# Two chained transformer blocks on one core: even start of the differential attention, earlier second scan, later last feed-forward product

## What is computed

```python
# first block, differential attention (8 heads, each with two score maps of width 64)
sc = jnp.einsum('bqhcd,bkhcd->bhcqk', qblk, k).astype(jnp.float32) * scale
p = jax.nn.softmax(sc, axis=-1)
w = (p[:, :, 0] - lambda_full * p[:, :, 1]).astype(v.dtype)
return jnp.einsum('bhqk,bkhe->bqhe', w, v)
# second block, one of its three branches (a gated linear scan, forward and backward)
q = jax.nn.silu(q_raw); f = lb + (1.0 - lb) * jax.nn.sigmoid(f_raw); k = (1.0 - lb) * jax.nn.sigmoid(-f_raw)
o_f = _hgrn2_scan(q, k[:, :, 0], v, log_f[:, :, 0])
o_b = _flip(_hgrn2_scan(_flip(q), _flip(k[:, :, 1]), _flip(v), _flip(log_f[:, :, 1])))
return _group_rmsnorm(o_f + o_b, norm_g, HG_H) * jax.nn.silu(g_out)
# second block, feed-forward
up = _dwconv(u @ w_up[l], ffn_conv_w[l], ffn_conv_b[l])
a_half, v_half = jnp.split(up, 2, axis=-1)
h = h + (jax.nn.silu(a_half) * v_half) @ w_down[l]
```

## Time and profile before

| | us |
|---|---|
| median of the 3 runs | 2515.18 (2513.99, 2515.18, 2522.87) |
| the profiled execution | 2519.92 |
| its span | 2518.1 |
| PE busy | 2456.8 (98%) |
| DVE, ACT, POOL busy | 1790.1 (71%), 1449.0 (58%), 258.8 (10%) |
| weights read from HBM | 424.4 MB, 170 GB/s over the span |

### The profile page before, as it was taken

One profiled execution on the slowest core, in us unless ns is written; L12 is line 12 of the kernel. 1 busy time (PEld: TensorE's weight loads), 2 busy tenths in 40 slices (PEclk: granted clock), 3 DMA queues, 4 the chain that ended last, 5 costly groups with the idle time before them and its releaser, 6 DMA issues.

```text
span 2518.1 us, 42226 instructions
## 1 busy us (share of the span) xinstructions
PE 2456.8 (98%) x17296; PEld 2255.5 (90%) x17296; DVE 1790.1 (71%) x2897; ACT 1449.0 (58%) x2122; POOL 258.8 (10%) x222
## 2 busy tenths in 40 slices
PE   8999999999999999899999999999999999999998
PEld 8888999888889898799999799998898999899997
DVE  5567675565576755587868887885597778887875
ACT  5547555445465554477565655664766656556654
POOL 0000002000000000000113720000010106500000
PEclk9999999999999999899999999999999999999999
DMA  7543476655434566554466645555554467645663
GB/s 258 152 135 119 159 249 194 203 180 157 130 117 151 184 194 202 161 151 128 125 198 191 196 136 190 186 183 194 154 152 125 138 196 204 184 151 183 192 207 127
DMA packets 358916, 430.44 MB, mean 171 GB/s; under 512 B 20616, under 2 KB 286310, under 8 KB 358468
## 3 DMA queue, kind: packets, MB, share of 16 engines
q1 hardware_dynamic: 341312, 401.72, 51.1%
q10 hardware_dynamic: 14340, 14.93, 2.6%
q0 software_dynamic: 3072, 11.10, 1.4%
HBM read 424.44 MB, written 3.24 MB: 170 GB/s over the span
## 4 chain that ended last, share of the span: by engine, by line
PE 88%; DVE 7%; ACT 3%; issue 1%; DMA 1%; POOL 0%; POOLq 0%; ACTq 0%; DVEq 0%
PE ps L112 85%; PE ps L115 2%; DVE wlo L121 1%; ACT L118 1%; ACT hgKm L118 1%; ACT whi L118 0%; ACT E L118 0%; ACT lnv L118 0%; DVE hgQB L121 0%; DMA kT<-in_diff_lambda 0%; DVE hgQF L121 0%; DVE E L124 0%; DVE sbc L130 0%; DVE E L133 0%; DVE hgKm L121 0%
## 5 line engine op out<-in xcount | busy, mean ns | idle before, releaser
L121 DVE TENSOR_TENSOR wlo<-wring,whi 128x1024 fp32r<-128x1024 f32 (+1 forms) x768 | 920.2, 1218 | 257.0 <-ACT whi L118 256.2
L118 ACT ACTIVATE whi<-wring 128x1024 fp32r<-128x1024 f32 (+1 forms) x768 | 802.8, 1054 | 431.3 <-PE ps L112 405.2
L112 PE MATMUL ps<-uT,whi 128*128 128x256 f32 x4640 | 822.2, 281 | 6.7 <-DVE wlo L121 5.0
L112 PEld LDWEIGHTS ps<-uT,whi 128*128 128x128 f32 x4640 | 706.7, 188 | 16.1 <-DVE wlo L121 8.2
L112 PE MATMUL ps<-uT,wlo 128*128 128x256 f32 x2320 | 646.8, 279 | 0.0
L112 PEld LDWEIGHTS ps<-uT,wlo 128*128 128x128 f32 x2320 | 438.9, 189 | 0.0
L112 PE MATMUL ps<-xT,whi 128*128 128x256 f32 x2112 | 378.1, 283 | 2.5 <-DVE xT L121 1.3
L112 PEld LDWEIGHTS ps<-xT,whi 128*128 128x128 f32 x2112 | 321.8, 188 | 10.2 <-issue 6.2
L112 PE MATMUL ps<-xT,wlo 128*128 128x256 f32 x1056 | 294.6, 279 | 0.0
L112 PE MATMUL ps<-whi,hid 128*128 128x512 f32 x864 | 270.4, 392 | 1.6 <-DVE wlo L121 1.6
L112 PEld LDWEIGHTS ps<-xT,wlo 128*128 128x128 f32 x1056 | 198.2, 188 | 0.3
(11 more groups left out here) (395 smaller groups left out, 3570.6 us busy)
## 6 DMA issues: line engine op xcount, KB each, us to landing
wring<-in_w_in SPq DMA_DIRECT2D x346, 512.0 KB, 4.2
wring<-in_mlp_w SPq DMA_DIRECT2D x128, 512.0 KB, 4.3
wring<-in_w_up SPq DMA_DIRECT2D x88, 512.0 KB, 4.5
wring<-in_w_down SPq DMA_DIRECT2D x44, 512.0 KB, 4.4
wring<-in_w_branch SPq DMA_DIRECT2D x32, 512.0 KB, 3.3
wring<-in_w_out SPq DMA_DIRECT2D x32, 512.0 KB, 4.5
wring<-in_mem_w_kv SPq DMA_DIRECT2D x16, 512.0 KB, 6.3
wring<-in_w_br_hg SPq DMA_DIRECT2D x16, 512.0 KB, 5.2
```

The source lines that it names most:

```text
L112: return self.e.matmul(*p, **k) if self.e else Nothing()
L118: return self.e.activation(*p, **k) if self.e else Nothing()
L121: return self.e.tensor_tensor(*p, **k) if self.e else Nothing()
```

## The change

The second argument `even` makes `staged` yield also for a stage that has nothing yet; `diff` uses it and yields once more ahead of it. `by_panels` hides a generator's yields that made no panel. `hg_proj` makes the `GG` panels before those of `GI` and queues the last `forget_scale` behind the first of them. `hg_scan(0)` takes the second scan as `following` and calls three of its steps (start and split; first product and merge; scale and products of level 0) between its own last ones; the first scan and the projection are woven at 1.22 and 1 by panels, the second scan and the two gates at 1.1 and 1 by panels. `hgscaled` becomes four events, one for each operand, and ACT's and POOL's copies of a merge wait each for their own. The first product goes from PSUM to `hgA` by ACT (`hg_first`) instead of DVE. `hg_start` of the second scan waits for the first scan's products of level 6, `hg_split` for its cross product; the squares of the first scan use `B0.kf` instead of `QK[0][1]`. In the feed-forward two panels of the down projection are made ahead of the last `ffn_product` (2 + 12 steps instead of 14).

```diff
@@ -328,7 +328,8 @@
-def staged(n, *stages):
+def staged(n, *stages, even=False):
@@ -336,6 +337,8 @@
                     yield
+            elif even and rest and i < lag:
+                yield
@@ -467,6 +470,14 @@
+    def by_panels(g):
+        n = len(panels)
+        for _ in g:
+            if len(panels) > n:
+                n = len(panels)
+                yield
@@ -731,8 +742,9 @@
                     sq.freed = raw.freed = (c.oD.name, h - 1)
+            yield
             yield from staged(8, (scores(0), 0, True), (scores(1), 0, True), (lambda h: turn_unit(un[h, 0]), 1, True), (values, 2, True),
-                              (norm, 3, False), (weights, 0, False), (gain, 4, False))
+                              (norm, 3, False), (weights, 0, False), (gain, 4, False), even=True)
             ar.give(qT, kT, dv, *rings[0], *rings[1])
@@ -998,13 +1010,16 @@
             yield from projB(w, GF + 1024 + c0, 512, uT, forget(B.b, B.kb, 8 + hf * 4))
+            B.g = ar.take("hgg", 1024, at=o + 6144)
+            to_g = projB(w, GG + c0, 512, uT, features_to(B.g, ACT.Silu))
+            next(to_g)
+            do("forget_scale", *pend.pop())
+            yield
+            yield from to_g
             B.v = ar.take("hgv", 1024, at=o + 5120)
             yield from projA(w, GI + c0, 512, uT, tokens_to(B.v, 512))
-            do("forget_scale", *pend.pop())
-            B.g = ar.take("hgg", 1024, at=o + 6144)
-            yield from projB(w, GG + c0, 512, uT, features_to(B.g, ACT.Silu))
-        def hg_scan(hf, B, W):
+        def hg_scan(hf, B, W, following=None):
             B.tag, B.c, B.hf, B.sq = ("hg", l, hf), c, hf, {}
@@ -1014,8 +1029,8 @@
             do("hg_merge", B, 0)
+            do("hg_first", B, us)
             yield
-            do("hg_level", B, -1, us)
             for j in range(7):
@@ -1030,9 +1045,13 @@
             yield
-            yield
+            if not hf:
+                some(following, 1)
+                yield
             def values(h):
-                B.sq[h] = W.sq.take()
+                B.sq[h] = W.sq[hf].take()
                 do("hg_values", B, c, h, AB.take(), yh)
@@ -1057,7 +1081,8 @@
             W.QK = [[ar.take("hgQm", 1024, at=13824 + 2048 * i), ar.take("hgKm", 1024, at=14848 + 2048 * i)] for i in range(2)]
-            W.sq = Slots([Buf("hgsq", 0, 512, W.QK[0][1].ap[:, o:o + 512]) for o in (0, 512)])
+            W.sq = [Slots([Buf("hgsq", 0, 512, b.ap[:, o:o + 512]) for o in (0, 512)]) for b in (B0.kf, W.QK[0][1])]
             W.A4 = W.At.ap.rearrange("p (s h t) -> p s h t", s=2, h=4)
@@ -1200,14 +1225,15 @@
         W, yh = hg_work(), ar.take("yh", 2048, at=25104)
-        weave((hg_scan(0, B0, W), 1), (hg_proj(1, B1), 1.3))
+        second = hg_scan(1, B1, W)
+        weave((hg_scan(0, B0, W, second), 1.22), (by_panels(hg_proj(1, B1)), 1))
 ...
             yield from gates([1])
-        weave((hg_scan(1, B1, W), 1), (two_gates(), 1))
+        weave((second, 1.1), (by_panels(two_gates()), 1))
         ar.give(*W.QK[0])
@@ -1301,10 +1327,12 @@
             run(projB(a["w_up_2"][l], DFF2 + k0 * 128, 256, uT, out_v(k0)))
+        down = projA(a["w_down_2"][l], 0, 1024, hid, add_to_h(("h2", l)))
+        some(down, 2)
         do("ffn_product", hid, *f.wait)
         ar.give(uT, fc, *aslots, *vslots)
-        down = projA(a["w_down_2"][l], 0, 1024, hid, add_to_h(("h2", l)))
-        some(down, 14)
+        some(down, 12)
@@ -1557,7 +1585,7 @@
     def hg_cross(B, us):
-        e.wait_ge(*at(("hgscaled", B.tag, 6)))
+        e.wait_ge(*at(("hgscaled", B.tag, 6, "kb")))
         for st, k, q in ((0, B.kf, B.W.QF), (1, B.kb, B.W.QB)):
@@ -1565,7 +1593,7 @@
                 m = e.matmul(p3[:, h, :], k4[:, h, st * 128:st * 128 + 128], q4[:, h, 128 - st * 128:256 - st * 128], start=True, stop=True)
-            m.then_inc(*up("pe_level", u.full))
+            m.then_inc(*up("pe_level", u.full, *([("hgcross", B.tag)] if st else [])))
@@ -1903,14 +1931,27 @@
             e.wait_ge(*at(("hgprod", B.tag, j - 2)))
-            e.wait_ge(*at(("hgscaled", B.tag, j - 1)))
+            e.wait_ge(*at(("hgscaled", B.tag, j - 1, "QF")))
         else:
 ...
         e.activation(halves(Qm, 1, n), halves(B.W.QF, 1, n), ACT.Copy).then_inc(*up("act_hg", ("hgQF", B.tag, j)))
+        if j >= 1:
+            e.wait_ge(*at(("hgscaled", B.tag, j - 1, "kf")))
         e.activation(halves(Km, 0, n), halves(B.kf, 0, n), ACT.Copy)
+        if j >= 1:
+            e.wait_ge(*at(("hgscaled", B.tag, j - 1, "kb")))
         e.activation(halves(Km, 1, n), halves(B.kb, 1, n), ACT.Copy).then_inc(*up("act_hg", ("hgK", B.tag, j)))
+    def hg_first(B, us):
+        if B.last:
+            e.wait_ge(*at(("yhraw", B.last, 2)))
+        for st in range(2):
+            e.wait_ge(*at(us[st].full))
+            e.activation(B.W.A4[:, st, :, st * 128:st * 128 + 128], us[st].ap.rearrange("p (h t) -> p h t", h=4), ACT.Copy).then_inc(
+                *up("act_hg", us[st].key, ("hglevel", B.tag, st, -1)))
@@ -2462,7 +2503,7 @@
         if B.last:
-            e.wait_ge(*at(("yh", B.c.l, B.hf * 4 - 1)))
+            e.wait_ge(*at(("hgprod", B.last, 6)))
         for x in (B.kf, B.kb):
@@ -2473,17 +2514,14 @@
             p3 = u.ap.rearrange("p (h t) -> p h t", h=4)
-            if j < 0:
-                if B.last:
-                    e.wait_ge(*at(("yh", B.c.l, B.hf * 4 - 1)))
-                e.tensor_copy(d, p3).then_inc(*up("dve_level", u.key, ("hglevel", B.tag, st, j)))
-                continue
             mask = cst[:, C_M + 128 * j:C_M + 128 * j + 128].bitcast(U32).rearrange("p (h t) -> p h t", h=1).to_broadcast([128, 4, 128])
 ...
         W = B.W
+        if B.last:
+            e.wait_ge(*at(("hgcross", B.last)))
         for k in (0, 2):
@@ -2497,13 +2535,12 @@
         e.wait_ge(*now("dve_hg"))
-        for x, side, T, ev in ((W.QF, 1, Tf, "hgQF"), (B.kf, 0, Tf, "hgK"), (W.QB, 0, Tb, "hgQB"), (B.kb, 1, Tb, "hgK")):
+        for x, side, T, ev, name in ((W.QF, 1, Tf, "hgQF", "QF"), (B.kf, 0, Tf, "hgK", "kf"), (W.QB, 0, Tb, "hgQB", "QB"), (B.kb, 1, Tb, "hgK", "kb")):
             e.wait_ge(*at((ev, B.tag, j)))
-            o = e.tensor_tensor(half(x, side), half(x, side), tb(T, 1 - side), ALU.mult)
+            e.tensor_tensor(half(x, side), half(x, side), tb(T, 1 - side), ALU.mult).then_inc(*up("dve_hg", ("hgscaled", B.tag, j, name)))
         if j < 6:
             e.tensor_tensor(W.Tf[j % 2].ap[:, 0:nb], tp(Tf, 0), tp(Tf, 1), ALU.mult)
-            o = e.tensor_tensor(W.Tb[j % 2].ap[:, 0:nb], tp(Tb, 0), tp(Tb, 1), ALU.mult)
-        o.then_inc(*up("dve_hg", ("hgscaled", B.tag, j)))
+            e.tensor_tensor(W.Tb[j % 2].ap[:, 0:nb], tp(Tb, 0), tp(Tb, 1), ALU.mult).then_inc(*up("dve_hg"))
@@ -2759,7 +2796,7 @@
             e.wait_ge(*at(("hgprod", B.tag, j - 2)))
-            e.wait_ge(*at(("hgscaled", B.tag, j - 1)))
+            e.wait_ge(*at(("hgscaled", B.tag, j - 1, "QB")))
         else:
```

More of the change, by code:

```diff
@@ L2041, in scalar_program @@
                  merged=merged, ln_stats=ln_stats, ln_out=ln_out, relu_square=relu_square, square_part=square_part, square_rows=square_rows, rms_scale=rms_scale, small_gates=small_gates,
-                 cumsum_rows=cumsum_rows, store_rows=store_rows, store_max=store_max, spread_rows=spread_rows, ml_max_cols=ml_max_cols, forget_out=forget_out, hg_merge=hg_merge, hg_cross=hg_cross,
+                 cumsum_rows=cumsum_rows, store_rows=store_rows, store_max=store_max, spread_rows=spread_rows, ml_max_cols=ml_max_cols, forget_out=forget_out, hg_merge=hg_merge, hg_first=hg_first, hg_cross=hg_cross,
                  hg_values=hg_values, hg_norm=hg_norm, ssd_conv=ssd_conv, ssd_silu=ssd_silu, ssd_turn=ssd_turn,
```

## The result

The changed kernel takes 2494.78 us (median of 2489.87, 2491.52, 2498.04 and 2499.91) against 2517.15 of the kernel before, run beside it: ratio 0.9909, 95% interval 0.9883 to 0.9935. The forecast of 18.5 is near their middle, but they differ by more than one interval allows, and what makes them differ is part of this case.

What follows compares the result with a forecast made beforehand. PE was taken as the bound, busy 2456.8 of 2518.1 us. Attention 2.5, scans 10.2, feed-forward 1.6 and clock 4.2 sum to 18.5, so the median falls from 2515.2 to 2496.7 us; range 2487 to 2508.

Steps and rivals of the forecast that it cites:

- The sum: Whole kernel: attention 2.5, scans 10.2, feed-forward 1.6 and clock 4.2 us, together 18.5 us less.
- Attention's start: Transposes of head 1, each layer: the wait of 2.07 us becomes 0.6; 2.5 us saved in both layers.
- Its end: Attention's end: from head 2 on the old pattern, one block later, so the two waits of 0.6 us stay.
- The first scan: First scan, each layer: waits of 0.69 and 0.22 us go, as events shorten the chain; PE's work between levels unchanged.
- POOL's copy: First scan's merge: the copy can start at 1131.5, takes 0.62 to 1.59 us, ends by 1133.1 at the latest.
- Rival 2: Scans: chain not short enough, POOL's copy slowed beside DVE; 5.1 + 2.8 us come back, 2504.6 us; chance 0.10.
- The second scan: Second scan, each layer: waits of 1.59 us at its start and 2.57 at level 1 go, by starting earlier.
- The feed-forward: Third down panel: waits of 0.81 and 0.79 us for its low part go; 1.6 us saved.
- rival 3: First weave: DVE becomes the bound, kernel slower by 9.2 us, 2524 us; chance 0.04.
- The clock: After the scans' waits: three half-clock stretches of 3.4 us go, at 1.4 us each; 4.2 us saved.
- rival 1: Later stages: moved waits may set another PE pace; 2504 us if worse (chance 0.13), 2491 if better (0.10).
- The sign that the prediction named: Up projections: another pace, seen in matmul counts of 50 us, would show the forecast wrong; before, 426 and 444.

## Why the prediction was right, and where its steps were not

**The sum.** 18.5 us were forecast; three comparisons gave 22.4, 14.6 and 19.0. From span to span (2518.1 to 2488.1, 2497.8 and 2496.9) the profiles part the 30.0, 20.3 and 21.2 us into idle 15.9, 15.4, 15.2; half clock, that at the norms included, 6.6, 4.5 and 5.2; pace 5.7, -0.1 and -0.8. 0.5 to 1.8 us are left over. The waits were forecast at 14.3 and the clock at 4.2, so both terms hold and both are a little low. Part of this rest may be that a group behind a wait takes longer itself (1.91 us for 15 products behind a wait, 1.84 without), which was not tried by itself. That the first comparison's time hit the forecast within 2 us is in part luck: its gain was 3.9 us larger than forecast, and its kernel before 2.0 us slower than the runs that the forecast started from.

**Attention's start: right in size.** 0.49 in the first profile, 0.49 to 0.71 over all with the even start, for the estimate of 0.6. **Its end: wrong.** "The two of 0.6 near the end of the attention stay": they went, 1.3 us. The step that failed is "from head 2 on the pattern is the old one, one block later": the units of head 6 changed place against the panels, as the rows above show, and the even start alone does it. PE has the same 5.4 us of work between the last scores and the last transposes in both kernels; it is ACT's last exponential that comes 0.8 us sooner behind those scores. That this follows from head 6's place is what the order of the queues suggests; no run varied it alone.

**The first scan: right result, half the cause.** "PE's work between them is the same, and only the chain gets shorter": the events do take both waits, by themselves, but the chain need not get shorter. The spacing changes where DVE's low parts stand against a scale, and with it the events are not needed. Counting panels between products on PE alone hid that; the same count has to be made on DVE's queue. The copies of the first product, moved to ACT, were costed as DVE's saving and not as part of the cure: by the first weave alone 0.13 us is left, and the 1.2 us that they free at level 1 more than cover it.

**POOL's copy: mis-sized.** 1.59 us was taken as the end; runs show up to 3.85. Rival 2's mechanism is real, and with the events alone it eats all they bring. In the changed kernel it costs nothing: no product waits, with two or three panels between most levels of the second scan, and not because the copy is short.

**The second scan: right result, half the cause.** All 10.2 us of the scans went. But 6.0 of them (hgKm 10.2 before; 3.7 on ACT and 0.5 on DVE with the first weave alone) go by spacing the first weave's panels, and the early start adds about 3 over a late one.

**The feed-forward** was right: 1.6 us, no new wait. **DVE as the bound** (rival 3): 75.4 of 83 us busy where 73.7 were forecast, and no wait.

**The clock: right in kind, its price too low.** The stretch in the earlier trace rows was read as 19 matmuls; that count takes in those already under way and those behind, and 16 start within it, against 30 at full clock. So it cost 1.7 us, not 1.4. Over all profiles PE waited 2 us or more 20 times at the attention's start or in the scans, and 17 times a stretch at half clock came within or about 1 us behind the wait; at the same places in the seven profiles of changed kernels, where no wait there is over 0.8, none did in 28. Six profiles have the wait of the earlier trace rows at 187 to 190, and four of them a stretch with it; why the one in the earlier trace rows had none stays open. One of the four stretches gone in the first profile (561.8) had no wait ahead, and comes again in other runs.

**The pace** (rival 1): rightly a matter of some 6 us, wrongly laid to the change. The sign that the prediction named did come (444 matmuls for 426 in the up projection of layer 0), but other profiles of unlike kernels have it as well. The range needed it for another reason: executions of one program differ by it.

## What to carry to other kernels

When two queues are woven, count the steps that the slower helper engine has ahead of the critical one, not only the panels between two products on the busy engine; spacing them evenly did more here than a finer event or an earlier start. Before a copy is started earlier on GpSimd, look at what VectorE does at that moment. And where the gain is below 1%, judge by the waits of several profiles: one execution's pace can be worth as much as a part of the change.

## What was not expected of the hardware

The same program runs stretches of its fp32r matmuls (128x256) at 113.3 or at 117.8 ns from start to start, at a granted clock of 1.00, and which stretch has which differs between executions: 16.2, 22.0 and 22.7 us of excess in three profiles of one program. The cause stays open; no run here varied it.

GpSimd's copy of 128x512 numbers took 0.61 to 3.85 us by what VectorE did beside it, and a multiplication of VectorE 1.13 us instead of 0.69 beside such a copy. Half-clock stretches of 3.4 us also come with no wait ahead: four runs have one at 53 us, and five at 557 to 564.
